# Turning an expert's gathered tokens by transposing DMAs instead of on the matrix engine

## The chip, the core and the metric

The kernel runs on one core of a Trainium2 chip. The core has a matrix engine (PE, with PEld for its weight loads), a vector engine (DVE), a scalar engine (ACT), GpSimd (POOL) and a queue engine (SP), beside 16 DMA engines that they share. PE writes only to PSUM, and other engines copy from there to SBUF. The metric is the device time of one execution in microseconds (us), here the median over several executions.

## The reference

One layer of a diffusion backbone over 2048 tokens of width 1024: a token mixer (convolution heads and HGRN heads), and then a mixture of 16 experts in which each expert picks its 256 best tokens. Only the mixture is touched:

```python
gate, idx = lax.top_k(probs.transpose(0, 2, 1), cap)          # cap = 256, 16 experts
xs = jax.vmap(lambda hb, ib: hb[ib])(h, idx)                  # gathered token rows
hid = (jax.nn.silu(jnp.einsum('becd,edf->becf', xs, p['w_gate']))
       * jnp.einsum('becd,edf->becf', xs, p['w_up']))
out = jnp.einsum('becf,efd->becd', hid, p['w_down']) * gate[..., None].astype(h.dtype)
y = ...zeros((n, d)).at[ib.reshape(-1)].add(ob.reshape(-1, d))
```

## The kernel before

Every float32 product is made of three bf16 products (`triple`, lines 89 to 91): each operand is split in a high half (`hi`, the value rounded to bf16) and a low half (`lo`, what is left over). The token rows lie in HBM as `s_rows`: per token 1024 bf16 high halves, 1024 bf16 low halves and the router's 16 probabilities.

`moe_stage` runs the experts one after another. Each engine has its own program; the first expert and the last are written out (`experts`, `peeled`), and those between are a loop. Engines meet through counters (semaphores) alone. For one expert:

- POOL gathers its 256 rows from `s_rows` into `mrows` (`rows`, two halves `s` of 128 tokens) by two indirect DMAs, about 45 us ahead of their use, and at the end adds the expert's output to `s_y` in HBM by two indirect DMAs (L2294), one for each `s`.
- PE needs the rows with the model width on the partitions. `turn` (L2558) does this for the next expert in two calls: 16 transposes of 128x128 each (L2565) into the PSUM tiles `ptx[0]` (high) and `ptx[1]` (low), after which ACT copies `ptx[0]` into `xhi` (L2325) and DVE copies `ptx[1]` into `xlo` (L2435). `xhi` and `xlo` exist once, so their new contents may be written only after the last gate/up product of the expert that runs (counter `gu_ps`).
- PE runs eight gate/up steps `f` (48 products `pgu` of 256 columns each, L89 to L91) and then four down steps `q` (24 products `pd` of 512 columns each, L2608 to L2610). The first call of `turn` stands after step f = 6, the second after q = 0.
- ACT applies tanh (`thb`, L2345), and ACT and DVE make `fhi` and `flo` of the hidden values. DVE weighs the output (`ysb`, L2467).
- The weights are six blocks `b` of 2 MB in float32 (gate, up, gate, up, down, down), loaded by SP (L2011) into three staging buffers `mwst`. ACT rounds each half block into `mwhi` (L2337), DVE subtracts into `mwlo` (L2440), and after the second half of a block the staging buffer is free and SP may load the block three further on. Blocks 0 to 2 of an expert are loaded and split while the one before it runs. SP therefore issues block 3 of an expert during the down steps of the expert before it, and block 4 a little later.

SP's program is one queue in program order, and each issue waits for its counter:

```python
for b in range(NB):
    wait(sp, w_lo[b % NS], 2 * (e * 2 + b // NS))
    EW.load(sp, e, b)
```

Of the kernel before, what the change touches and what calls it, by code (L numbers as in the profile page):

```python
# [27 lines left out]
P = 128  # L28
# [2144 lines left out]
def moe_stage(nc, K, I, scr, EW, out):  # L2173
# [5 lines left out]
    with nc.cleanup_on_exit(), ExitStack() as ctx:  # L2179
# [30 lines left out]
        oh0_ok, ls_ok = m.sem("oh0_ok"), m.sem("ls_ok")  # L2210
        oh_ok, id_ps, idf_ok, id_ok, idc_ok, gt_ok = (m.sem("oh_ok"), m.sem("id_ps"), m.sem("idf_ok"), m.sem("id_ok"),
                                                      m.sem("idc_ok"), m.sem("gt_ok"))
        got, tx_ps, tx_ok = m.sem("got"), m.sem("tx_ps"), m.sems("tx_ok", 2)
        gu_ps, mth_ok, sg_ok, hid_ok, fhi_ok, flo_ok = (m.sem("gu_ps"), m.sem("mth_ok"), m.sem("msg_ok"), m.sem("hid_ok"),
                                                        m.sem("fhi_ok"), m.sem("flo_ok"))
        d_ps, y_ok, put = m.sem("d_ps"), m.sem("my_ok"), m.sem("put")
# [22 lines left out]
        with nc.Block() as block:  # L2239
            @block.sync  # L2240
            def _(sp):
                def one(e):
                    for b in range(NB):
                        if b < NS and isinstance(e, int) and e == 0:
                            continue
                        if b == NS and isinstance(e, int) and e == 0:
                            wait(sp, got, 32)
                        wait(sp, w_lo[b % NS], 2 * (e * 2 + b // NS))
                        EW.load(sp, e, b)
                peeled(sp, NE, one)  # L2250

                def row_group(g):
                    for t in range(4 * g, 4 * g + 4):
                        sp.dma_start(row_tile(t), scr["y"][t * P:(t + 1) * P, :]).then_inc(yt_in[g], 16)

                sp.dma_start(fg[:], I["final_g"].partition_broadcast(P)).then_inc(fg_in, 16)
                wait(sp, put, LAST * 32)
                for g in range(2):
                    wait(sp, w_lo[g], 2 * (LAST * 2 + 2))
                    row_group(g)  # L2260
                wait(sp, gu_ps, LAST * 8 + 4)
                row_group(3)
                wait(sp, w_lo[2], 2 * (LAST * 2 + 2))
                row_group(2)

            @block.gpsimd
            def _(pool):
                pool.dma_start(g2[:], scr["modrows"][6:8, :].rearrange("a n -> (a n)").partition_broadcast(P))\
                    .then_inc(g2_in, 16)
                nc.gpsimd.memset(pflag[:], 0.0).then_inc(fl_ok, 1)  # L2270

                def carrier():
                    nc.gpsimd.tensor_tensor(pflag[:], pflag[:], pflag[:], ALU.mult).then_inc(fl_ok, 1)  # L2273

                def prep(e, first=False):
                    wait(pool, fl_ok, 1 if first else e * 3 - 1)
                    wait(pool, id_ok, e + 1)
                    wait(pool, tx_ps, e * 4)
                    wait(pool, gt_ok, e)
                    carrier()  # L2280
                    for s in range(2):
                        pool.indirect_dma_start(out=rows32[:, s, :], out_offset=None, in_=scr["rows"],
                                                in_offset=bass.IndirectOffsetOnAxis(ap=idn[:, s:s + 1], axis=0))\
                            .then_inc(got, 16)

                def body(e, nxt):
                    if nxt:
                        prep(e + 1)
                    wait(pool, put, e * 32)
                    for s in range(2):  # L2290
                        wait(pool, y_ok, e * 4 + 2 * s + 2)
                        wait(pool, fl_ok, e * 3 + s + (3 if nxt else 2))
                        carrier()
                        pool.indirect_dma_start(out=scr["y"], out_offset=bass.IndirectOffsetOnAxis(ap=idc[:, s:s + 1], axis=0),  # L2294
                                                in_=ysb[:, s, :], in_offset=None, compute_op=ALU.add).then_inc(put, 16)

                def last(e, nxt):
                    wait(pool, put, e * 32)
                    for s in range(2):
                        pool.indirect_dma_start(out=ygat[:, s, :], out_offset=None, in_=scr["y"],  # L2300
                                                in_offset=bass.IndirectOffsetOnAxis(ap=idn[:, s:s + 1], axis=0))\
                            .then_inc(yg_in, 16)
                    for n, t in enumerate(ORDER):
                        wait(pool, yt_ok, n + 1)
                        pool.dma_start(out[0, t * P:(t + 1) * P, :], row_tile(t)).then_inc(yt_out, 16)
                    wait(pool, yt_out, 16 * NT)
                    for s in range(2):
                        wait(pool, yn_ok, 2 * s + 2)
                        pool.indirect_dma_start(out=out_rows, out_offset=bass.IndirectOffsetOnAxis(ap=idn[:, s:s + 1], axis=0),
                                                in_=ygat[:, s, :], in_offset=None).then_inc(yg_out, 16)  # L2310

                out_rows = out.rearrange("a t d -> (a t) d")
                def prep0(e):
                    prep(0, True)
                    EW.first_low(nc, pool, HEAD_START - 2)

                experts(pool, prep0, body, last)
                wait(pool, yg_out, 32)

            @block.scalar  # L2320
            def _(act):
                def turn(e, j):
                    wait(act, tx_ps, e * 4 + 2 * j + 1)
                    wait(act, gu_ps, e * 8)
                    nc.scalar.activation(xhi[:, 4 * j:4 * j + 4, :], ptx[0][:], ACT.Copy).then_inc(tx_ok[0], 1)  # L2325

                def split(e, r):
# [51 lines left out]
                def body(e, nxt):  # L2379
                    for j in range(8):  # L2380
                        hidden(e, j, nxt)
                        if not nxt and j >= 4:
                            row_squares(2 * j - 8)
                            row_squares(2 * j - 7)
                    for q in range(4):
                        if nxt:
                            if q < 2:
                                turn(e + 1, q)
                            split(e, HEAD_START + 8 + q)
                        else:  # L2390
                            for n in range(8 + 4 * q, min(NT, 12 + 4 * q)):
                                row_squares(n)
                            gathered_squares(q)
                            if q % 2 == 1:
                                gathered_deviation(q // 2)

                def prep0(e):
                    turn(0, 0)
                    turn(0, 1)

                experts(act, prep0, body)

# [1 line left out]
            def _(dve):  # L2404
# [24 lines left out]
                    nc.vector.scalar_tensor_tensor(idn[:], f2[:, :, 1], float(P), f2[:, :, 0], ALU.mult, ALU.add)\  # L2429
                        .then_inc(id_ok, 1)  # L2430

                def turn(e, j):
                    wait(dve, tx_ps, e * 4 + 2 * j + 2)
                    wait(dve, gu_ps, e * 8)
                    nc.vector.tensor_copy(xlo[:, 4 * j:4 * j + 4, :], ptx[1][:]).then_inc(tx_ok[1], 1)  # L2435

                def split(e, r):
# [62 lines left out]
                def body(e, nxt):  # L2500
# [17 lines left out]
                    wait(dve, gt_ok, e + 1)  # L2518
                    for q in range(4):
                        if nxt:  # L2520
                            if q < 2:
                                turn(e + 1, q)
                            split(e, HEAD_START - 1 + 8 + q)
                        else:
                            for n in range(4 + 4 * q, min(NT, 8 + 4 * q)):
                                row_scaled(n)
# [6 lines left out]
                def prep0(e):  # L2533
                    first_list()
                    numbers(0)
                    list_rows(nc, dve, K, 1, NE, ls_ok, 0)
                    turn(0, 0)
                    turn(0, 1)

                experts(dve, prep0, body)  # L2540

# [1 line left out]
            def _(pe):  # L2543
# [11 lines left out]
                        last = nc.tensor.matmul(pid, oneh[:, t, :], Re[:, t, :], start=(t == 0), stop=(t == NT - 1))  # L2555
                    last.then_inc(id_ps, 1)

                def turn(e, j):  # L2558
                    wait(pe, got, e * 32 + 32)
                    for part in range(2):  # L2560
                        wait(pe, tx_ok[part], e * 2 + j)
                        for k in range(4):
                            for s in range(2):
                                c = part * D + (4 * j + k) * P
# [3 lines left out]

                def body(e, nxt):
                    start = isinstance(e, int) and e == 0  # L2570
                    for part in range(2):
                        wait(pe, tx_ok[part], e * 2 + (1 if start else 2))
                    for f in range(8):
                        h, jj = f // 4, f % 4
                        if jj == 0:
# [17 lines left out]
                        last.then_inc(gu_ps, 1)  # L2593
                        if nxt and f == 2:
                            token_list(e + 1)
                        if nxt and f == 6:
                            turn(e + 1, 0)
                    wait(pe, flo_ok, e * 8 + 7)
                    for b in (4, 5):
                        wait(pe, w_lo[b % NS], 2 * (e * 2 + b // NS + 1))  # L2600
                    for q in range(4):
# [8 lines left out]
                            last = nc.tensor.matmul(pd[q % 2][:], fl, whi[:, 4 + c, k, :], start=False,  # L2610
                                                    stop=(k == KD - 1))
                        last.then_inc(d_ps, 1)
                        if nxt and q == 0:
                            turn(e + 1, 1)

                def prep0(e):
                    token_list(0)
                    turn(0, 0)
                    turn(0, 1)

                experts(pe, prep0, body)

# [83 lines left out]
```

## Time and profile before

| | |
|---|---|
| median of 3 runs | 2312.58 us |
| lowest and highest of the runs | 2309.34 and 2317.04 us |
| span of the profiled execution | 2315.0 us, within the runs' range |
| PE busy, DVE busy, ACT busy | 94%, 70%, 45% of the span |
| moved by the DMA engines | 377.14 MB, mean 163 GB/s |
| mean granted clock of PE | 0.971 of full speed |

The span runs from the first to the last instruction of one execution, recorded by the profiler; the record gives no other time for that execution, and the span lies 2.4 us above the median of the runs. Busy time is the union of an engine's instructions; a busy PE isn't PE at its peak, since its products overlap.

### The profile page before, as it was taken

The numbers are of one execution on the slowest core, as the hardware profiler recorded it, in microseconds if no ns is written. First come the engines' busy times: TensorE is split into PE (matmuls) and PEld (weight loads), VectorE is DVE, ScalarE is ACT, GpSimd is POOL, SyncE is SP. The second block draws the span as 40 slices with busy tenths as digits, with TensorE's granted clock in tenths as the row PEclk, the third lists the DMA queues.
The fourth block names the chain that finished last, engine by engine and source line by source line (L and its number), as shares of the span: only waits on it lengthen the run. The fifth ranks groups of instructions, "written<-read, shape, count | busy, mean of one in ns | idle before, by whom it ended". The sixth has DMA issues, their size and how long they took to land. (4 is left out here: it accounts for less than half of the span.)

```text
span 2315.0 us, 38576 instructions
## 1 busy us (share of the span) xinstructions
PE 2187.4 (94%) x14737; PEld 1480.7 (64%) x14885; DVE 1609.4 (70%) x2233; ACT 1041.0 (45%) x1329; POOL 504.9 (22%) x537
## 2 busy tenths in 40 slices
PE   7799999998999999899986999999999999999995
PEld 3444444444878787755534777777777777777773
DVE  2749999785679687865566667666666666666666
ACT  3611011456566666644442444543444444543444
POOL 1710001013657567300012111101111011101111
PEclk9899999999999999899977999999999999999998
DMA  9341002454021111375453776667766766667776
GB/s 345 98 73 37 14 23 87 149 161 124 6 55 50 45 57 24 116 263 165 152 189 137 241 232 230 224 218 227 243 220 211 242 218 240 219 221 233 229 233 266
DMA packets 216931, 377.14 MB, mean 163 GB/s; under 512 B 38147, under 2 KB 79619, under 8 KB 216333
## 3 DMA queue, kind: packets, MB, share of 16 engines
q1 hardware_dynamic: 198702, 317.38, 40.7%
q0 software_dynamic: 16528, 56.47, 9.0%
q10 hardware_dynamic: 1616, 2.16, 0.3%
q8 instruction: 53, 0.87, 0.2%
q14 instruction: 32, 0.26, 0.0%
HBM read 313.44 MB, written 62.54 MB: 162 GB/s over the span
## 5 line engine op out<-in xcount | busy, mean ns | idle before, releaser
L89 PE MATMUL pgu<-xhi,mwhi 128*128 128x256 bf16 x2048 | 558.8, 273 | 0.0
L90 PE MATMUL pgu<-xlo,mwhi 128*128 128x256 bf16 x2048 | 558.7, 273 | 0.0
L91 PE MATMUL pgu<-xhi,mwlo 128*128 128x256 bf16 x2048 | 558.6, 273 | 0.0
L2440 DVE TENSOR_TENSOR mwlo<-mwst,mwhi 128x2048 bf16<-128x2048 f32 x187 | 427.0, 2283 | 0.0
L2337 ACT ACTIVATE mwhi<-mwst 128x2048 bf16<-128x2048 f32 x186 | 350.8, 1902 | 0.1
L2345 ACT ACTIVATE thb<-pgu 128x256 f32<-128x256 f32 x128 | 49.0, 383 | 548.0 <-PE pgu L91 548.0
L676 DVE SCALAR_TENSOR_TENSOR co<-u,taps,co 128x1984 f32<-128x1984 f32 (+22 forms) x120 | 234.1, 1951 | 3.7
L2451 DVE SCALAR_TENSOR_TENSOR thb<-thb,pgu 128x256 f32<-128x256 f32 x128 | 53.8, 421 | 259.0 <-ACT thb L2345 259.0
L2273 POOL TENSOR_TENSOR mpflag<-mpflag 1x1 f32<-1x1 f32 x46 | 37.5, 815 | 846.4 <-DVE ysb L2467 579.4
L89 PEld LDWEIGHTS pgu<-xhi,mwhi 128*128 128x128 bf16 x2048 | 200.5, 98 | 24.6
L90 PEld LDWEIGHTS pgu<-xlo,mwhi 128*128 128x128 bf16 x2048 | 200.6, 98 | 24.5
L91 PEld LDWEIGHTS pgu<-xhi,mwlo 128*128 128x128 bf16 x2048 | 200.5, 98 | 23.5
L2610 PE MATMUL pd<-mwhi,flo 128*128 128x512 bf16 x511 | 193.9, 379 | 0.8
L2609 PE MATMUL pd<-mwlo,fhi 128*128 128x512 bf16 x497 | 188.9, 380 | 2.9 <-DVE flo L2459 1.4
L2608 PE MATMUL pd<-mwhi,fhi 128*128 128x512 bf16 x481 | 182.9, 380 | 3.3 <-DVE ysb L2467 3.1
L1521 PEld LDWEIGHTS pout<-E,KX 128*128 128x128 f32 (+2 forms) x1024 | 151.3, 181 | 32.6 <-POOL KX L1100 8.4
L1521 PE MATMUL pout<-E,KX 128*128 128x32 f32 (+2 forms) x1024 | 145.1, 234 | 13.0 <-POOL KX L1100 8.0
L2467 DVE SCALAR_TENSOR_TENSOR ysb<-pd,gate,g 128x512 f32<-128x512 f32 x64 | 47.9, 749 | 84.5 <-PE pd L2610 84.5
L1498 PE MATMUL pj<-hhi,wst 128*128 128x512 bf16 (+1 forms) x300 | 104.0, 372 | 1.6 <-PEq L422 1.6
L1498 PE MATMUL pout<-hhi,wst 128*128 128x512 bf16 (+1 forms) x284 | 95.8, 364 | 0.2
L557 ACT ACTIVATE jb<-pout 128x512 f32<-128x512 f32 (+1 forms) x54 | 31.4, 591 | 136.9 <-PE pout L91 119.6
L1308 DVE TENSOR_TENSOR_SCAN B<-segm,E 128x512 f32<-128x512 f32 (+1 forms) x40 | 52.1, 1303 | 58.6 <-ACT E L1156 58.6
(397 smaller groups left out, 4399.2 us busy)
## 6 DMA issues: line engine op xcount, KB each, us to landing
mwst<-in_w_gate SPq DMA_DIRECT2D x32, 2048.0 KB, 9.1
mwst<-in_w_up SPq DMA_DIRECT2D x32, 2048.0 KB, 7.9
mwst<-in_w_down SPq DMA_DIRECT2D x32, 2048.0 KB, 7.9
wst<-in_w_in SPq DMA_DIRECT2D x28, 512.0 KB, 6.1
big<-in_ada_w SPq DMA_DIRECT2D x5, 2048.0 KB, 14.6
s_rows<-row SPq DMA_DIRECT2D x16, 520.0 KB, 5.8
u<-in_ada_w SPq DMA_DIRECT2D x8, 1024.0 KB, 6.1
xt<-in_x SPq DMA_DIRECT2D x16, 512.0 KB, 4.4
```

The lines of the kernel that those rows point to most:

```text
L89: nc.tensor.matmul(out, lh, rh, start=(first and k == 0), stop=False)
L90: nc.tensor.matmul(out, lh, rl, start=False, stop=False)
L91: ins = nc.tensor.matmul(out, ll, rh, start=False, stop=(last and k == n - 1))
L676: nc.vector.scalar_tensor_tensor(o, i, taps[:, c, k:k + 1], o, ALU.mult, ALU.add).then_inc(tap_ok, 1)
L1498: ins = nc.tensor.matmul(pj[i % 2][:, 0:n], w, x, start=(mm == 0), stop=(mm == 3 * KD - 1))
L1521: ins = nc.tensor.matmul(pat[0:keys, n * CH:(n + 1) * CH], KX[:, p, n * P:n * P + keys], E[:, p, n * CH:(n + 1) * CH], start=True, stop=True)
L2337: nc.scalar.activation(whi[:, b, ks], wst[:, b % NS, ks], ACT.Copy).then_inc(w_hi, 1)
L2440: nc.vector.tensor_tensor(wlo[:, b, ks], wst[:, b % NS, ks], whi[:, b, ks], ALU.subtract)\
L2451: nc.vector.scalar_tensor_tensor(thb[:, p], thb[:, p], 1.0, pgu[p][:, 0, :], ALU.add, ALU.mult)\
L2608: nc.tensor.matmul(pd[q % 2][:], fh, whi[:, 4 + c, k, :], start=(k == 0), stop=False)
L2609: nc.tensor.matmul(pd[q % 2][:], fh, wlo[:, 4 + c, k, :], start=False, stop=False)
L2610: last = nc.tensor.matmul(pd[q % 2][:], fl, whi[:, 4 + c, k, :], start=False, stop=(k == KD - 1))
```

## The change

For the first expert nothing changes. For experts 1 to 15, PE's two calls of `turn`, ACT's two copies into `xhi` and DVE's two copies into `xlo` are taken out. In their place SP issues four transposing DMAs (`turned`): each reads 128 tokens by 1024 bf16 values (256 KB) of `mrows` and writes them turned into `xhi` or `xlo`, SBUF to SBUF. They stand in SP's queue right behind the load of block 3 of that expert and ahead of the loads of blocks 4 and 5. They wait for the gather of the expert (`got`) and for the last gate/up product of the expert before it (`gu_ps`). PE starts the gate/up steps when all four have landed (`xt_in`, 64 counts for an expert), and POOL overwrites `mrows` only after that.

```diff
             @block.sync
             def _(sp):
+                def turned(e):
+                    wait(sp, gu_ps, e * 8)
+                    sp.sem_inc(x_free, 1)
+                    sp.wait_ge(x_free, 1)
+                    for part, x in enumerate((xhi, xlo)):
+                        for s in range(2):
+                            sp.dma_start_transpose(x[:, :, s * P:(s + 1) * P], rows[:, s, part * D:(part + 1) * D])\
+                                .then_inc(xt_in, 16)
+
                 def one(e):
                     for b in range(NB):
                         if b < NS and isinstance(e, int) and e == 0:
                             continue
-                        if b == NS and isinstance(e, int) and e == 0:
-                            wait(sp, got, 32)
+                        if b == NS:
+                            wait(sp, got, e * 32 + 32)
                         wait(sp, w_lo[b % NS], 2 * (e * 2 + b // NS))
                         EW.load(sp, e, b)
+                        if b == NS and not (isinstance(e, int) and e == 0):
+                            turned(e)
                 peeled(sp, NE, one)
...
                 def prep(e, first=False):
-                    wait(pool, tx_ps, e * 4)
+                    if not first:
+                        wait(pool, tx_ps, 4)
+                        wait(pool, xt_in, e * 64 - 64)
...
                     for q in range(4):
                         if nxt:
-                            if q < 2:
-                                turn(e + 1, q)
                             split(e, HEAD_START + 8 + q)
...
                 def body(e, nxt):
                     start = isinstance(e, int) and e == 0
-                    for part in range(2):
-                        wait(pe, tx_ok[part], e * 2 + (1 if start else 2))
+                    if start:
+                        for part in range(2):
+                            wait(pe, tx_ok[part], 1)
+                    else:
+                        wait(pe, xt_in, e * 64)
...
                         if nxt and f == 2:
                             token_list(e + 1)
-                        if nxt and f == 6:
-                            turn(e + 1, 0)
...
                         last.then_inc(d_ps, 1)
-                        if nxt and q == 0:
-                            turn(e + 1, 1)
```

(The `turn` calls are taken out of ACT's and of DVE's loop over `q` in the same way.)

SP's queue in the experts' loop, from the load of block 3 (`in_w_up`) to the end of the loop. Before:

```order
L2011 DMA mwst<-in_w_gate 128x8x512
L75 ISA
L2011 DMA mwst<-in_w_up 128x8x512
L2011 DMA mwst<-in_w_down 128x8x512 x2
L81 REGISTER_ALU
L81 COMPARE_AND_BRANCH
```

And now:

```order
L2011 DMA mwst<-in_w_up 128x8x512
L75 REGISTER_ALU
L2249 DMA_TRANSPOSE xhi<-mrows 128x8x128 x2
L2249 DMA_TRANSPOSE xlo<-mrows 128x8x128 x2
L2011 DMA mwst<-in_w_down 128x8x512 x2
L81 REGISTER_ALU
L81 COMPARE_AND_BRANCH
```

The four transposing DMAs lie between the loads of block 3 and block 4.

DVE's program in the same loop, from the last `flo` of an expert to the weighing of the second down step. Before:

```order
L2459 TENSOR_TENSOR flo<-hb,fhi 128x256
L75 ISA
L75 REGISTER_ALU
L2435 COPY xlo<-ptx 128x1024
L75 REGISTER_ALU
L2440 TENSOR_TENSOR mwlo<-mwst,mwhi 128x2048
L75 REGISTER_ALU
L2467 SCALAR_TENSOR_TENSOR ysb<-pd,gate,g 128x512
L75 REGISTER_ALU
L2435 COPY xlo<-ptx 128x1024
L75 REGISTER_ALU
L2440 TENSOR_TENSOR mwlo<-mwst,mwhi 128x2048
```

And now:

```order
L2469 TENSOR_TENSOR flo<-hb,fhi 128x256
L75 REGISTER_ALU
L2450 TENSOR_TENSOR mwlo<-mwst,mwhi 128x2048
L75 REGISTER_ALU
L2477 SCALAR_TENSOR_TENSOR ysb<-pd,gate,g 128x512
L75 REGISTER_ALU
L2450 TENSOR_TENSOR mwlo<-mwst,mwhi 128x2048
```

Both copies of `xlo` are gone, and the subtraction that frees the staging buffer for block 3 (the first `mwlo` here) follows `flo` at once.

## Rows read from the trace of the kernel before

**Rows 1.** The page: PE's busy tenths and granted clock, 40 slices.
```profile
PE   7799999998999999899986999999999999999995
PEclk9899999999999999899977999999999999999998
```

**Rows 2.** Busy time of each engine in one expert's period (stretches).
```profile
core 0: us, PE busy (x) PEld busy (x) DVE busy (x) ACT busy (x) POOL busy (x), PEclk, DMA share, GB/s
1376.10:1441.00 64.90, 64.74 (x528) 49.15 (x529) 42.62 (x48) 29.03 (x30) 7.70 (x8) 1.00 0.69 226
```

**Rows 3.** Chain that ended last, in order of time: start, us, what.
```profile
1289.58 0.89 PE ptx L2565 x16
1300.89 0.89 PE ptx L2565 x16
...
2197.20 0.89 PE ptx L2565 x16
2208.51 0.89 PE ptx L2565 x16
```

**Rows 4.** Timeline of ACT around one expert's end: start, us, instruction, idle before.
```profile
1414.04 0.38 ACT L2345 ACTIVATE thb<-pgu 128x256 f32<-128x256 f32 x1 [2.75 <-PE pgu L91]
...
1419.28 0.38 ACT L2345 ACTIVATE thb<-pgu 128x256 f32<-128x256 f32 x1 [2.75 <-PE pgu L91]
...
1425.41 0.38 ACT L2345 ACTIVATE thb<-pgu 128x256 f32<-128x256 f32 x1 [3.65 <-PE pgu L91]
...
1452.55 1.90 ACT L2337 ACTIVATE mwhi<-mwst 128x2048 bf16<-128x2048 f32 x1
...
1463.03 1.90 ACT L2337 ACTIVATE mwhi<-mwst 128x2048 bf16<-128x2048 f32 x1
```

**Rows 5.** Timeline of DVE at the same expert's end.
```profile
1428.83 0.42 DVE L2459 TENSOR_TENSOR flo<-hb,fhi 128x256 bf16<-128x256 f32 x1
1429.16 0.68 DVE L2435 COPY xlo<-ptx 128x1024 bf16<-128x1024 bf16 x1
1429.76 2.28 DVE L2440 TENSOR_TENSOR mwlo<-mwst,mwhi 128x2048 bf16<-128x2048 f32 x1
...
1437.34 2.28 DVE L2440 TENSOR_TENSOR mwlo<-mwst,mwhi 128x2048 bf16<-128x2048 f32 x1
```

**Rows 6.** Timeline of SP: issues of block 3 (up) and block 4 (down).
```profile
1432.07 0.37 SPq L2011 DMA_DIRECT2D mwst<-in_w_up  x1
1439.64 16.52 SPq L2011 DMA_DIRECT2D mwst<-in_w_down  x2
```

**Rows 7.** Stretches, columns as in rows 2, while block 3 loads.
```profile
1436.00:1438.00 2.00, 2.00 (x11) 0.91 (x10) 1.33 (x2) 1.46 (x1) 0.41 (x1) 1.00 1.05 406
1438.00:1440.00 2.00, 2.00 (x11) 0.94 (x10) 1.61 (x1) 0.00 (x0) 1.84 (x2) 1.00 0.60 223
```

**Rows 8.** DMA issues from 1432 to 1433 us: size, us to landing.
```profile
mwst<-in_w_up SPq DMA_DIRECT2D x1, 2048.0 KB, 7.9
```

**Rows 9.** Timeline of PE: a late product of q = 0, the first of the next expert.
```profile
1429.74 0.38 PE L2608 MATMUL pd<-mwhi,fhi 128*128 128x512 bf16 x1
...
1446.83 0.27 PE L89 MATMUL pgu<-xhi,mwhi 128*128 128x256 bf16 x1
```

**Rows 10.** DMA queues from 685 to 692 us: packets, MB, share of 16 engines.
```profile
DMA packets 1056, 0.26 MB, mean 37 GB/s; under 512 B 1056, under 2 KB 1056, under 8 KB 1056
q1 hardware_dynamic: 1056, 0.26, 17.6%
```

**Rows 11.** POOL's first scatter; its queue's first packets, 1444.5 to 1445.5 us.
```profile
1439.82 1.62 POOL L2294 DMA_INDIRECT s_y<-ysb,idc  x1 [0.16 <-issue]
...
q0 software_dynamic: 14, 0.06, 32.1%
```

**Rows 12.** DMA issues of the whole span: size, median us to landing.
```profile
s_v<-jb POOLq DMA_DIRECT2D x18, 256.0 KB, 2.7
...
cc<-in_c SPq DMA_DIRECT2D x1, 4.0 KB, 1.7
```

More of the change, by code:

```diff
@@ L2212, in moe_stage @@
                                                       m.sem("idc_ok"), m.sem("gt_ok"))
-        got, tx_ps, tx_ok = m.sem("got"), m.sem("tx_ps"), m.sems("tx_ok", 2)
+        got, tx_ps, tx_ok, xt_in = m.sem("got"), m.sem("tx_ps"), m.sems("tx_ok", 2), m.sem("xt_in")
+        x_free = m.sem("x_free")
         gu_ps, mth_ok, sg_ok, hid_ok, fhi_ok, flo_ok = (m.sem("gu_ps"), m.sem("mth_ok"), m.sem("msg_ok"), m.sem("hid_ok"),
@@ L2321, in _, with turn @@
             def _(act):
-                def turn(e, j):
-                    wait(act, tx_ps, e * 4 + 2 * j + 1)
-                    wait(act, gu_ps, e * 8)
+                def turn(j):
+                    wait(act, tx_ps, 2 * j + 1)
                     nc.scalar.activation(xhi[:, 4 * j:4 * j + 4, :], ptx[0][:], ACT.Copy).then_inc(tx_ok[0], 1)
@@ L2397, in prep0 @@
                 def prep0(e):
-                    turn(0, 0)
-                    turn(0, 1)
+                    turn(0)
+                    turn(1)
                 experts(act, prep0, body)
@@ L2430, in numbers, with turn @@
                         .then_inc(id_ok, 1)
-                def turn(e, j):
-                    wait(dve, tx_ps, e * 4 + 2 * j + 2)
-                    wait(dve, gu_ps, e * 8)
+                def turn(j):
+                    wait(dve, tx_ps, 2 * j + 2)
                     nc.vector.tensor_copy(xlo[:, 4 * j:4 * j + 4, :], ptx[1][:]).then_inc(tx_ok[1], 1)
@@ L2520, in body @@
                         if nxt:
-                            if q < 2:
-                                turn(e + 1, q)
                             split(e, HEAD_START - 1 + 8 + q)
@@ L2536, in prep0 @@
                     list_rows(nc, dve, K, 1, NE, ls_ok, 0)
-                    turn(0, 0)
-                    turn(0, 1)
+                    turn(0)
+                    turn(1)
                 experts(dve, prep0, body)
@@ L2556, in token_list, with turn @@
                     last.then_inc(id_ps, 1)
-                def turn(e, j):
-                    wait(pe, got, e * 32 + 32)
+                def turn(j):
+                    wait(pe, got, 32)
                     for part in range(2):
-                        wait(pe, tx_ok[part], e * 2 + j)
+                        wait(pe, tx_ok[part], j)
                         for k in range(4):
@@ L2612, in body @@
                         last.then_inc(d_ps, 1)
-                        if nxt and q == 0:
-                            turn(e + 1, 1)
                 def prep0(e):
                     token_list(0)
-                    turn(0, 0)
-                    turn(0, 1)
+                    turn(0)
+                    turn(1)
                 experts(pe, prep0, body)
```

## The prediction

> **What bounds the kernel now.** The page comes first: from the 23rd slice on, the experts, PE is busy in nine tenths and more of every slice at nine tenths and more of the full clock [rows 1]. The stretch of one expert's period says the same closer: PE is busy 64.74 of 64.90 us, DVE 42.62, ACT 29.03, and the DMA engines have a share of 0.69 [rows 2]. So whatever is taken off PE there is gained, as long as nothing new makes PE wait. The chain of work in order of time then shows the pieces that the change removes on that very path: 16 transposes at a time, 0.89 us, the first at 1289.58 and the last at 2208.51 us, two for each of experts 1 to 15, 30 pieces in all [rows 3].
>
> **What is removed.** ACT's tanh follows each gate/up step, so its starts are PE's step: 5.24 us from 1414.04 to 1419.28 and 6.13 us over the step with a turn in it, 0.89 more [rows 4]. This agrees with the chain, so I take 30 x 0.89 = 26.7 us, 1.78 us for each expert. ACT's two copies and DVE's two aren't on the path. They are worth nothing by themselves, but one of them stands ahead of the subtraction that frees the staging buffer, which matters below: from 1429.16 to 1429.76, 0.60 us [rows 5].
>
> **What is added, and when it can start.** I put the new DMAs on the time axis of the expert shown. SP issues block 3 at 1432.07 [rows 6], when DVE has ended the subtraction of 1429.76 [rows 5]. After the change the first turn (0.89) lies no longer ahead of it, nor does DVE's copy (0.60): block 3 is issued at 1430.6. The last gate/up product, for which `turned` also waits, is over by then (tanh of the last step starts at 1425.41 [rows 4]), and so is the gather. SP goes on to the four transposing DMAs at about 1431. Their packets stand behind those of block 3 in SP's queue. That load saturates the DMA engines (share 1.05, 406 GB/s), and its packets end at about 1439.2 (0.60 of the stretch from 1438 on) [rows 7]; it lands 7.9 us after its issue, at 1440.0 [rows 8], 0.8 after its last packet. Moved by 1.49 us, its packets end at 1437.7, and the turning begins there.
>
> **When it is needed.** The next expert's first product starts at 1446.83 [rows 9], and after the change 1.78 earlier, at 1445.05. With 0.8 us for landing, the turning of 1 MB (4 x 256 KB) may last T = 1445.05 - 0.8 - 1437.7 = 6.5 us before PE waits. Each us beyond costs 15 us in all, and at T = 8.3 the whole gain is used up.
>
> **How long the turning takes.** The trace has no transposing DMA, so T is bounded. From below: at the rate of the weight loads, 406 GB/s [rows 7], 1.05 MB take 2.6 us. From above: if every DMA were paid alone, with nothing overlapped, 4 x 2.7 us as the 256 KB DMAs land [rows 12], 10.8 us. If it were paid in its 32 blocks of 128x128, each as the smallest DMA in the trace, 1.7 us [rows 12], 54 us. Between them stand the smallest packets that SP's queue moves: 1056 packets of about 256 bytes take 17.6% of 16 engines for 7 us, 18.7 ns each [rows 10]. A row of a 128x128 block of bf16 is just such a piece, 256 bytes, and 1 MB is 4096 of them, 256 on each engine: 4.8 us. I take T = 4.8 us, by that nearest row. The turning then ends at 1442.5 and lands at 1443.3, 1.7 us before PE needs it. Against the load of block 3 itself nothing is lost, as it stands in front.
>
> The rows give a moved MB between 2.6 and 4.8 us, by the size of its packets. The Trainium skill (Advanced Engine Details and Errata, X-Bar Transpose (TRN2)) says that transposing DMAs are as fast as regular ones and expects 350 to 400 GB/s; by that T would be an estimated 2.6 to 3.0 us, and the sum would be the same, with more to spare. No transposing DMA in this trace can show whether it holds.
>
> **What lies beside it.** The other work of the DMA engines is POOL's first scatter: it is issued at 1439.82, but its packets show only from 1444.5 on [rows 11], 1442.7 after the change. So a turning of 4.8 us is just over when they come; a longer one has to share. Behind the turning in SP's queue waits block 4, issued at 1439.64 when the subtraction of 1437.34 is over [rows 5, 6], now due at 1437.9. Even if SP is held until 1443.3, block 4 lands some 8 us later at 1451.3, and ACT first reads it at 1463.03 - 1.78 = 1461.3 [rows 4]: 10 us to spare. Block 3 is read from 1452.55 on [rows 4] and lands at 1438.5. The engines' DMA share rises from 0.69 [rows 2] by 4.8 of 63 us, to about 0.8 of the shorter period. On PE the next cover is thin but unmoved: the last `flo` ends at 1429.25 [rows 5], and the product group that needs it starts at 1429.74 [rows 9]; the turn that goes stands ahead of both, and the copies that go stand behind. All this costs nothing.
>
> **The sum.** 2315.0 - 26.7 = 2288.3 us for the profiled execution. Its span lies 2.4 us above the median of the runs, so for the median 2312.6 - 26.7 = 2285.9 us, 1.2% faster.
>
> **The rivals.**
> - A short stall, chance 0.16: T lies between 6.5 and 8.3 us or a little above, because the turning's packets are dearer than plain ones or because its end meets the scatter. For it speaks how near all the times lie to each other (1.7 us); against it that the scatter comes late. At T = 7.4 PE waits 0.9 us for each expert: 2285.9 + 15 x 0.9 = 2299 us.
> - The four DMAs don't overlap, chance 0.20, and this is the one that ends on the other side. Each 256 KB transfer is paid with its landing, 2.7 us [rows 12], and the first can only start when block 3 has landed at 1438.5: 1438.5 + 10.8 = 1449.3, a wait of 4.3 us at the first product. 2285.9 + 15 x 4.3 = 2350 us. It decides from a wait of 1.78 us on, so from 2.1 us for each of the four. For it speaks that a turned block can't be written before its rows are all read; against it that plain DMAs of one queue follow each other with no gap: the engines are at 1.05 share in the middle of a load [rows 7].
> - Turning block by block, chance 0.10. 32 blocks of 128x128, each at 1.7 us [rows 12], end at 1437.7 + 54 = 1491.7, a wait of 47 us for each expert and 2990 us in all; SP is held too, and blocks 4 and 5 come late inside the same wait. Against it speaks that each instruction carries 128x1024 values and so should be spread over the engines as any other. The Trainium skill (VectorE: DVE Perf Modes, The three transpose paths) gives 1309 ns for a 128x128 block by DMA against 390 ns on TensorE, and its Rules for kernel authors prefer TensorE where PSUM will do; if that price were paid 32 times, it would be an estimated 42 us for an expert and some 2810 us in all. That TensorE's own price in this stream is far lower is what the trace shows: 0.89 us for 16 of them, 56 ns each [rows 3].
> - No gain at all, chance 0.02: the time taken off PE comes back as another wait. PE has no other wait in the period that could grow (0.16 us idle of 64.90 [rows 2]), so this needs a cover that I have missed.
>
> **How the numbers follow.** The likeliest case, hidden turning, has 0.52; its own range is the runs' spread about 2286, 2281 to 2292 us. The whole range takes in the short stall and most of the four DMAs one by one (2350 at the full 2.7 us, less if they overlap in part): 2280 to 2348 us, with the lower parts of the second rival some 0.82. What is left out is the rest of it and the block-by-block case. Within 0.3% of before (2306 to 2320, about what a measurement can tell from no change) means a wait of 1.3 to 2.2 us: 0.05 of the short stall and the 0.02 of no gain, 0.07. Faster: 0.52 + 0.09 of the short stall = 0.61. Slower: 0.02 of it, 0.20 and 0.10, 0.32.
>
> **What would show it.** Right: no `ptx` in the experts' loop, a period of 63.0 us instead of 64.8, the four transposing DMAs issued at once behind block 3 and landing within 13 us of their issue, and no idle time ahead of an expert's first `pgu` product. A wait of PE there, put down to SP's DMAs, would show the rivals, and its length says which: under 2 us, about 4, or tens. The step that I trust least is T. If PE's clock falls after such waits, they cost more than their length: it shows 0.7 in the two slices ahead of the experts, where PE isn't full either [rows 1].

## The result, and the profile after

| | before | changed |
|---|---|---|
| median of 20 runs | 2313.35 us | 2322.3 us |
| lowest and highest | 2308.88, 2319.23 | 2312.59, 2330.18 |
| span of the profiled execution | 2315.0 us | 2313.3 us |

The ratio of the changed kernel to the one before is 1.0037, with a 95% interval from 1.0028 to 1.0046: slower by 0.4%, where 1.2% faster was forecast. The profiled execution of the changed kernel is one of its quickest (2315.06 us, when the median is 2322.3), so the profile shows the mechanism and not quite the median's amount of it.

The page of the changed kernel answers to [rows 1]: its PE line and its granted clock, unchanged to the eye in the experts' slices.

```profile
PE 2162.5 (93%) x14405; PEld 1446.0 (63%) x14405; DVE 1595.7 (69%) x2203; ACT 1013.5 (44%) x1299; POOL 505.6 (22%) x537
...
PE   7799999998999999899976999999999999999995
...
PEclk9899999999999999899987999999999999999998
```

PE has lost 24.9 us of busy time (2187.4 before), about what was taken away. The waits of PE, longest first in total, show where it went (waiting instruction, releaser, us in total, times, longest):

```profile
PE pgu L89 <- DMA xlo<-mrows: 27.7, 15, 2.7
```

Before there was no such line. Every one of the 15 experts now starts with a wait for the last turning DMA. One of them on PE's timeline (idle time and its releaser at the end of the row), which answers to [rows 9]:

```profile
1437.66 0.38 PE L2619 MATMUL pd<-mwhi,flo 128*128 128x512 bf16 x1
1439.62 0.28 PE L89 MATMUL pgu<-xhi,mwhi 128*128 128x256 bf16 x1 [1.59 <-DMA xlo<-mrows]
```

SP's and POOL's timelines at the same expert answer to [rows 6] and to the POOL row of [rows 11]:

```profile
1423.41 0.37 SPq L2011 DMA_DIRECT2D mwst<-in_w_up  x1
1423.99 7.69 SPq L2249 DMA_TRANSPOSE xhi<-mrows  x2
1431.72 4.43 SPq L2249 DMA_TRANSPOSE xlo<-mrows  x2
1436.26 12.71 SPq L2011 DMA_DIRECT2D mwst<-in_w_down  x2
```

```profile
1430.87 1.62 POOL L2308 DMA_INDIRECT s_y<-ysb,idc  x1 [0.16 <-issue]
```

The last product of the down steps starts at 1437.66, and in their pace (0.22 us from start to start) the next expert's first would have followed at 1437.9, 14.5 us after block 3's issue (1423.41), as the prediction's axis had it (1430.6 to 1445.05). The DMA queues in single microseconds (packets, MB, share of 16 engines; q1 is SP's queue, q0 POOL's), from 1432, 1434, 1435 and 1438 us on:

```profile
q1 hardware_dynamic: 1055, 0.26, 129.3%
...
q0 software_dynamic: 31, 0.13, 86.3%
q1 hardware_dynamic: 41, 0.01, 8.9%
...
q0 software_dynamic: 44, 0.18, 90.8%
q1 hardware_dynamic: 46, 0.01, 9.2%
...
q1 hardware_dynamic: 735, 0.25, 139.7%
```

At 1432 the turning moves 1055 packets of 256 bytes in a microsecond. Then the scatter's 4 KB packets come (from 1433.3 on), and the turning falls to 41 and 46 a microsecond, here about one for each packet of the scatter; at other experts of this trace it is fewer (from 1630.57 to 1631.57 it is 10 beside 49). At 1438 it is quick again. In all its packets last from 1430.6 to 1438.8, 8.2 us, of which some 3 are spent at this crawl.

### The profile page after: what moved, and what is told of

It is laid out like the page before. It is cut to its first block and busy times, and to the rows that moved or that the text cites. A ratio compares the mean times of both kernels' runs of the same rounds, so it can differ in the third digit from the quotient of the medians.

```text
span 2313.3 us, 37650 instructions
## 1 busy us (share of the span) xinstructions
PE 2162.5 (93%) x14405; PEld 1446.0 (63%) x14405; DVE 1595.7 (69%) x2203; ACT 1013.5 (44%) x1299; POOL 505.6 (22%) x537
## 5 line engine op out<-in xcount | busy, mean ns | idle before, releaser
L89 PE MATMUL pgu<-xhi,mwhi 128*128 128x256 bf16 x2048 | 559.1, 273 | 27.7 <-DMA xlo<-mrows 27.7
L2617 PE MATMUL pd<-mwhi,fhi 128*128 128x512 bf16 x512 | 194.6, 380 | 4.5 <-DVE ysb L2477 3.3
L2618 PE MATMUL pd<-mwlo,fhi 128*128 128x512 bf16 x512 | 194.6, 380 | 0.0
L1521 PEld LDWEIGHTS pout<-E,KX 128*128 128x128 f32 (+2 forms) x1024 | 146.4, 177 | 31.5 <-POOL KX L1100 7.7
L1498 PE MATMUL pout<-hhi,wst 128*128 128x512 bf16 (+1 forms) x304 | 101.4, 363 | 0.0
## 6 DMA issues: line engine op xcount, KB each, us to landing
mwst<-in_w_down SPq DMA_DIRECT2D x32, 2048.0 KB, 10.2
```

The source lines that it names most:

```text
L89: nc.tensor.matmul(out, lh, rh, start=(first and k == 0), stop=False)
L1498: ins = nc.tensor.matmul(pj[i % 2][:, 0:n], w, x, start=(mm == 0), stop=(mm == 3 * KD - 1))
L1521: ins = nc.tensor.matmul(pat[0:keys, n * CH:(n + 1) * CH], KX[:, p, n * P:n * P + keys], E[:, p, n * CH:(n + 1) * CH], start=True, stop=True)
L2617: nc.tensor.matmul(pd[q % 2][:], fh, whi[:, 4 + c, k, :], start=(k == 0), stop=False)
L2618: nc.tensor.matmul(pd[q % 2][:], fh, wlo[:, 4 + c, k, :], start=False, stop=False)
```

## The experiments

Each run gives the median, and the ratio to the kernel before with its 95% interval, from runs of both on the same chip, 4 to 10 executions of each run's kernel. Two theories for the wait were tested first: that the turning is hindered by the scatter, and that it is slow by itself.

**Without turning.** `turned` isn't issued, and the waits for it are gone.

```diff
-                        if b == NS and not (isinstance(e, int) and e == 0):
-                            turned(e)
...
-                    else:
-                        wait(pe, xt_in, e * 64)
```

> Leaves out the turning for experts 1 to 15: neither PE's transposes nor the DMAs, so experts 1 to 15 use the first expert's tokens. It prices what the change removes. Every theory expects the 30 x 0.89 us read from the chain: 2313 - 27 = 2286 us, a ratio to before of 0.988, and no wait of PE ahead of an expert's first product.

2285.65 us, ratio 0.9881 (0.9866 to 0.9897). The 26.7 us that the removed transposes were priced at are right to within the runs' spread.

**Scatter after the turning.** One wait is added on POOL, and nothing else is changed.

```diff
                     wait(pool, put, e * 32)
+                    wait(pool, xt_in, e * 64 + 64)
                     for s in range(2):
                         wait(pool, y_ok, e * 4 + 2 * s + 2)
```

> The change as it is, but POOL issues an expert's first scatter only after the next expert's turning has landed. Nothing else moves. Theory A (scatter against turning): the turning lands 4.8 + 0.8 us after block 3's last packets, about 1435.5, ahead of PE at 1438: PE's wait is gone, 2286 us, ratio to before 0.988. Theory B (the turning is slow by itself): nothing changes, PE waits about 1.8 to 2.5 us for each expert, 2315 to 2325 us.

2286.98 us, ratio 0.9887 (0.987 to 0.9904): the whole gain is there. Two stretches of its trace, columns as in [rows 2], from 1376 and from 1431 us on:

```profile
1376.00:1441.00 65.00, 65.00 (x516) 49.13 (x515) 42.14 (x48) 27.22 (x28) 7.00 (x10) 1.00 0.81 255
...
1431.00:1436.50 5.50, 5.50 (x28) 2.47 (x26) 3.27 (x3) 0.00 (x0) 0.00 (x0) 1.00 1.13 234
```

PE is never idle. The scatter is issued at 1437.82, and one microsecond of the turning, from 1433 on, shows the queue q1 alone:

```profile
1437.82 1.62 POOL L2309 DMA_INDIRECT s_y<-ysb,idc  x1 [0.52 <-issue]
```

```profile
q1 hardware_dynamic: 912, 0.23, 112.9%
```

Followed microsecond by microsecond, the 256-byte packets run from 7.3 to 12.2 us after block 3's issue (1424.18), with no scatter beside them: 4.9 us for 1 MB (4096 packets, so 836 in a microsecond in the mean), where 4.8 was forecast. The theory that the turning is slow by itself is gone.

**Everything twice.** As the last, with four more turning DMAs into a buffer that isn't read (`ygat`, idle until the end).

```diff
-                    for part, x in enumerate((xhi, xlo)):
+                    for part, x in ((0, xdup), (1, xdup2), (0, xhi), (1, xlo)):
```

> As the run with the later scatter, and each turning is done twice: four more transposing DMAs into a buffer that nobody reads, ahead of the four that count. It gives the price of 1 MB turned with no scatter beside it. Theory A (4.8 us for 1 MB): 9.6 us after block 3's packets, landing about 1440.2, a wait of 2.3 us for each expert, about 2320 us. Theory B (9 us for 1 MB): landing near 1449, a wait of 11 us for each expert, about 2450 us.

2378.53 us, ratio 1.0275 (1.0255 to 1.0295), 58 us more than the first theory's number and 72 less than the second's. The packets last 10.8 us for 2 MB, so 5.4 for 1 MB: near the first theory. PE's waits:

```profile
PE pgu L89 <- DMA xlo<-mrows: 60.0, 15, 4.8
```

They are 4.0 us for each expert, where the first theory said 2.3: that is 25 us of the 58. What it had left out beside that is PE's clock. Stretches behind one wait of 4.2 us, columns as in [rows 2] (the clock is the third number from the end):

```profile
1450.00:1454.00 4.00, 4.00 (x21) 1.77 (x19) 2.40 (x2) 0.00 (x0) 0.00 (x0) 1.00 1.02 194
1454.00:1458.50 4.50, 0.59 (x3) 0.09 (x1) 0.92 (x2) 0.00 (x0) 0.00 (x0) 0.94 1.03 173
1458.80:1462.80 4.00, 3.96 (x19) 2.87 (x20) 0.00 (x0) 0.00 (x0) 3.23 (x4) 0.50 1.05 376
1462.80:1466.80 4.00, 4.00 (x30) 3.20 (x29) 0.00 (x0) 0.00 (x0) 0.15 (x1) 0.76 1.04 252
1466.80:1470.80 4.00, 4.00 (x39) 3.59 (x38) 3.20 (x4) 2.49 (x3) 0.00 (x0) 1.00 0.69 136
```

After the idle stretch the clock is at half its level (1.2 instead of 2.4 GHz) for about 6 us, and PE starts 19 products where 39 fit. Before this, PE had worked at the full clock without a gap. From the first product behind this wait to the next expert's (1458.84 to 1528.88) there are 70.0 us, 7.0 more than the 63.05 without turning (64.83 - 1.78): the next wait is 4.0 of them, and the lower clock the other 3.0.

**Turning ahead of block 3.** The wait for the gather moves up to block 2's load, and `turned` ahead of block 3's.

```diff
-                        if b == NS:
+                        start = isinstance(e, int) and e == 0
+                        if b == (NS if start else NS - 1):
                             wait(sp, got, e * 32 + 32)
+                        if b == NS and not start:
+                            turned(e)
                         wait(sp, w_lo[b % NS], 2 * (e * 2 + b // NS))
                         EW.load(sp, e, b)
-                        if b == NS and not (isinstance(e, int) and e == 0):
-                            turned(e)
```

> The turning stands ahead of block 3's load in SP's queue (the wait for the gather stands a little earlier, ahead of block 2's load). Theory A (scatter against turning, 5 us for 1 MB by itself): SP issues the four DMAs as the last gate/up product ends, near 1417 on the axis of the changed kernel's expert, their packets follow block 2's at 1423 and end near 1428, before the scatter comes at 1433; no wait of PE, about 2286 us, ratio to before 0.988. Theory B (the four DMAs pay about 2.7 us each): packets end near 1434, also hidden, and 2286 us. Theory C (block 3 then lands too late for ACT, which reads it near 1445 on that axis): block 3's packets come 5 us later, end near 1436 and share with the scatter; 9 us to spare, so no cost expected; if it were late, ACT would wait for w_up.

2288.61 us, ratio 0.9876 (0.9856 to 0.9897). It beats both kernels and can't be told from the one with the later scatter. SP's timeline:

```profile
1417.89 0.37 SPq L2011 DMA_DIRECT2D mwst<-in_w_gate  x1
1419.49 6.55 SPq L2249 DMA_TRANSPOSE xhi<-mrows  x2
1426.09 2.69 SPq L2249 DMA_TRANSPOSE xlo<-mrows  x2
1428.96 0.44 SPq L2011 DMA_DIRECT2D mwst<-in_w_up  x1
```

SP is held for 9.3 us, and block 3 is issued at 1428.96. Its packets end near 1436.3, it lands 8.4 us after its issue, at 1437.4, and ACT first reads it at 1445.67, so the later load costs nothing, as expected.

**Turning behind block 4.** The condition `b == NS` at the call of `turned` becomes `b == NS + 1`.

> The turning stands behind block 4's load instead of block 3's: block 4 is issued near 1430.7 on the changed kernel's axis, its 2 MB (5.3 us alone) meet the scatter, and end near 1440; the turning's packets follow. Theory A: they end near 1445 and meet the second scatter (issued as the fourth down step is weighed, packets from about 1443 on), so they land between 1446 and 1450: a wait of 8 to 12 us for each expert against the need at 1438, plus the lower clock after such a wait (some 3 us as in the doubled run): 2286 + 15 x 13 = about 2480 us. A theory in which the place in the queue doesn't matter, because the chip moves the transposing DMAs' packets beside the loads', expects 2322 us as in the change.

2479.07 us, ratio 1.0712 (1.0687 to 1.0736); about 2480 was expected. The waits of PE:

```profile
PE pgu L89 <- DMA xlo<-mrows: 161.1, 15, 11.2
```

10.7 us for each expert, and the period is 12.9 us longer than without turning ((2479.07 - 2285.65) / 15); of the rest, 2.2 us, the clock is a part: it is granted at 0.61 in the 4 us behind the wait that ends at 1477.2, and at 1.00 from 1481.2 on. A place in the queue later by one 2 MB load is worth 10 us here against the changed kernel. One load alone is some 5 us; but block 4's load meets the first scatter, and the turning behind it the second, as was expected. In the microseconds from 1472 and 1473 on the turning is between its first packets (1469) and its last (1476):

```profile
q0 software_dynamic: 47, 0.19, 96.3%
...
q0 software_dynamic: 52, 0.20, 102.1%
q1 hardware_dynamic: 5, 0.00, 0.8%
```

In the first of them it moves no packet at all, so one for each of the scatter's is at most what it gets.

**ACT issues.** The four DMAs are issued by ACT behind its last `fhi`, in a queue of their own.

```diff
+                            if q == 0:
+                                turned(e + 1)
                             split(e, HEAD_START + 8 + q)
```

> ACT issues the four transposing DMAs, behind its last fhi of an expert, instead of SP; they then have a queue of their own and don't stand behind block 3. Theory A (a short packet has to wait for one long packet of the other queue): beside block 2's and block 3's 2 KB packets the turning goes at about a fifth of its rate, alone at its own 19 ns a packet; packets end near 1432, in time for PE. What it may cost is ACT itself: if the issuing engine is held while the DMAs queue, as SP is for 11 us in the change, ACT's splits of the next blocks come up to 11 us late, DVE's weighing stands behind them, and PE's down steps wait for it: 2290 to 2400 us, with ACT's DMA_TRANSPOSE rows long. If an engine is only held 1.3 us for each where nothing stands ahead in its queue, ACT loses 5.3 us, which its idle time before the next tanh covers: about 2286 us.

2334.19 us, ratio 1.0091 (1.0072 to 1.0111). PE's longest waits are now others:

```profile
PE pd L2617 <- DVE ysb L2477: 38.2, 17, 3.0
```

ACT's timeline, and DVE's and PE's first instruction that waited:

```profile
1425.11 3.54 ACTq L2331 DMA_TRANSPOSE xhi<-mrows  x1
1428.68 6.68 ACTq L2331 DMA_TRANSPOSE xlo<-mrows  x2
```

```profile
1437.41 2.29 DVE L2450 TENSOR_TENSOR mwlo<-mwst,mwhi 128x2048 bf16<-128x2048 f32 x1 [8.46 <-ACT mwhi L2348]
```

```profile
1440.42 0.39 PE L2617 MATMUL pd<-mwhi,fhi 128*128 128x512 bf16 x1 [2.66 <-DVE ysb L2477]
```

ACT is held from 1423.7 to 1435.4, its splits stand behind that, DVE's weighing behind them, and PE waits for the weighing: the first of the two outcomes that were foreseen for ACT. The queues beside each other (q1 is SP's, q10 now ACT's), in the microseconds from 1429, 1431, 1433 and 1435 on:

```profile
q10 hardware_dynamic: 1119, 0.28, 127.9%
...
q1 hardware_dynamic: 179, 0.37, 103.6%
...
q1 hardware_dynamic: 179, 0.37, 120.2%
q10 hardware_dynamic: 73, 0.02, 8.2%
...
q1 hardware_dynamic: 176, 0.36, 92.4%
q10 hardware_dynamic: 170, 0.04, 19.2%
```

Alone the turning moves 1119 packets in a microsecond. Beside the 2 KB packets of a weight load it passes about one for each of the load's from 1433.5 to 1436.5 (402 beside 429). But from 1430.25 to 1433.25 it moves none at all beside 457 of the load's, and none from 1424 to 1427, though its first DMA was issued at 1423.74 and its third at 1428.68. No run shows why. Theory A had expected a fifth of its rate all through and its last packet near 1432; it comes at 1438.6.

**Half rows.** Each scatter becomes two of 2 KB rows.

```diff
-                        pool.indirect_dma_start(... in_=ysb[:, s, :], in_offset=None, compute_op=ALU.add).then_inc(put, 16)
+                        for c in range(2):
+                            pool.indirect_dma_start(..., element_offset=c * SEG,
+                                                    in_=ysb[:, s, c * SEG:(c + 1) * SEG], ...).then_inc(put, 16)
```

> The change as it is, but each scatter is issued as two DMAs of half rows (2 KB instead of 4 KB for each token), so that the scatter's packets are half as long. Theory A (the two queues alternate packet by packet, so a short packet waits for one long one): while both are there, the turning passes one packet for each of the scatter's as before, but twice as many in a us, about 80 instead of 40 to 47; over the scatter's 4 us that wins some 0.4 us for each expert, and the time comes out between 2310 and 2322 us, unless POOL's two further issues (1.6 us each) put the scatter's first packets elsewhere. If POOL joins two half rows in one packet, nothing changes. A theory in which the scatter stops the turning altogether for its own length, whatever its packets, expects 40 to 47 packets a us and 2322 us.

2322.7 us, ratio 1.0047 (1.0026 to 1.0067), no change in time. The scatter's packets are now 2 KB (91 packets and 0.18 MB in one microsecond), but it comes in two parts, the second while the turning still runs or just after, and 54 packets of the turning beside those 91 are no clean sign of 80. Shorter stretches of the same trace show both: from 1571.28 to 1571.78 the turning passes 49 beside 45 (98 a microsecond, over twice the 41 to 46 beside 4 KB packets), from 1444.00 to 1444.75 only 23 beside 67 (31 a microsecond). The run doesn't settle whether the packets' length sets the pace, nor whether the two queues alternate at all.

**The changed kernel again**, for a second profile.

> The changed kernel again, for a second profile. Theory A: PE waits 1.5 to 3 us ahead of each expert, the turning's packets nearly stop for as long as the scatter's are there. Where the execution takes longer than the 2313.3 us span profiled first, the granted clock falls to half for some us after some of the waits, as it does behind each 4 us wait of the doubled run; if instead all the waits were just longer at a full clock, the clock is not part of it.

2323.8 us, ratio 1.0036 (1.0017 to 1.0055); the profiled span is 2325.0 us. PE's waits are nearly the same, but of the 15 stretches of 6 us behind each expert's first product two are at a lower clock, and in the first profile one (the stretches shown start 0.5 us behind that product):

```profile
PE pgu L89 <- DMA xlo<-mrows: 29.3, 15, 3.3
```

```profile
1382.95:1388.95 6.00, 6.00 (x58) 5.37 (x56) 0.57 (x2) 1.02 (x2) 0.87 (x1) 1.00 1.05 321
1449.46:1455.46 6.00, 6.00 (x33) 4.38 (x32) 0.00 (x0) 0.00 (x0) 0.00 (x0) 0.56 1.05 312
...
2102.94:2108.94 6.00, 6.00 (x42) 4.76 (x40) 0.00 (x0) 0.00 (x0) 0.79 (x1) 0.72 1.04 317
```

The clock fell after the longest wait of each profile, 2.7 us in the first (the first product at 2220.97) and 3.3 us in the second (1448.99), and after one of 2.0 us (2102.47). After the 27 other waits, of 1.3 to 2.2 us, it stayed at the full clock.

## Why the prediction was wrong

**What bounds the kernel, and what is removed: right.** 30 x 0.89 = 26.7 us came out as 27.5 in the run without turning (2313.17 - 2285.65).

**When it can start and when it is needed: right.** The turning's packets start 7.2 us after block 3's issue (7.1 forecast), and the next expert's first product would have started 14.5 us after it (14.45 forecast).

**How long the turning takes by itself: right.** 4.9 us with the scatter out of the way, 5.4 in the doubled run, against 4.8 from the 256-byte packets of [rows 10].

**What lies beside it: this step failed**, as it was put: "a turning of 4.8 us is just over when they come; a longer one has to share". Two things in it were wrong. The scatter's first packets came 2.2 to 3.7 us after its issue (the first scatters in the two profiles of the changed kernel; 2.4 at the one shown), not 4.7, so 0.9 to 2.4 us before a turning of 4.9 us was over. And sharing wasn't priced: I took it as slower by some share, when it stops the short packets almost wholly. The turning gets at most about one packet for each of the scatter's, and a packet of 256 bytes against one of 4 KB leaves it a twentieth of its pace for as long as the scatter lasts (41 to 46 against 836 in a microsecond): 8.2 us instead of 4.9. That is the "short stall" rival's mechanism with a larger size (its T of 7.4, and the 8.3 at which it put the break-even). It was given 0.16; that its end would meet the scatter was named there, but its price wasn't worked out, though the rows had it: q0's 14 packets in a third of 16 engines' microsecond [rows 11] are 0.37 us each, 20 times the 18.7 ns of a short one [rows 10]. A scatter's 128 rows of 4 KB are then 128 x 0.37 / 16 = 3.0 us of the engines' time by estimate, and the turning was stretched by 3.3: about the whole scatter. The run with the later scatter shows that the scatter is the whole cause of the wait. That the two queues alternate packet by packet isn't shown: beside the scatter and beside a load there were also whole microseconds with no packet of the turning.

**The sum.** From the chain, an expert's period before is 64.83 us ((2208.51 - 1300.89) / 14 [rows 3]) and 1.78 less without turning. In the two profiles of the changed kernel the first products of experts 1 and 15 lie 911.4 and 916.9 us apart, 65.1 and 65.5 us for each period, so the wait costs 2.1 and 2.5 us, more than the 1.78 gained. 15 x 0.3 = 5 us and 15 x 0.7 = 10 us frame the measured 9. By the prediction's own rule a turning of 8.2 us makes PE wait 8.2 - 6.5 = 1.7 us, 2311 us in all; so the mis-sized T brings the time back to that of before, and the last 11 us come on top. The bare waits (27.7 and 29.3 us in the rows) are a little longer than 15 x 1.7. In the first profile they are the whole difference from the run without turning (spans of 2313.3 and 2285.1 us). In the second a part is the clock: the two periods that begin with a lower clock are 67.5 and 66.8 us, 2.4 and 1.7 us above the usual 65.1. The last remark of the prediction, that the clock might fall after a wait, was right. What the rest of the median's 2322.3 us is made of isn't shown.

**The rivals.** Four DMAs one by one (2350 us) and block by block (2990 us) are refuted: 1 MB needs 4.9 us, not 10.8 or 54. SP being held was seen rightly as harmless (block 4 has 10 us to spare), and it is: with the later scatter SP is held for 10.2 us (12.2 in the changed kernel) and nothing is lost. On the rule of the Trainium skill (Advanced Engine Details and Errata, X-Bar Transpose (TRN2)), that transposing DMAs are as fast as regular ones, this case disagrees in the rate: 1 MB in 4.9 us is 214 GB/s, against 400 for the weight loads here and the 350 to 400 that the Trainium skill expects; it agrees with plain packets of the same 256 bytes. The other figure of the Trainium skill (VectorE: DVE Perf Modes, The three transpose paths), 1309 ns for a 128x128 block, isn't what a block costs in a row of them: 4.9 us for 32 are 153 ns each.

**What stays open.** Why the first scatter's packets come 2.2 to 3.7 us after its issue in the changed kernel and about 5 us after it before the change. Where a weight load ran at that time (before, without turning, turning ahead) it was 4.6 to 5.5 us; where short packets ran, less. In the changed kernel itself the second scatter of an expert, issued while block 4 loads, takes 4.2 to 5.5 us. No run varies this alone. Nor is it shown why the turning sometimes moves no packet beside another queue, and what decides whether the clock falls after a wait of 2 us.

## What to carry to other kernels

Before a transfer is called hidden, list what else is in the DMA engines in its window and how much of their time that work takes: a stream of 256-byte packets got at most about one for each packet of the other queue, so beside 4 KB packets it nearly stopped (41 to 46 in a microsecond, 1055 alone), and it ended 3.3 us late, by about the 3.0 us of the other transfer. The remedy was order and not speed: the same four DMAs one place earlier in the queue turned 0.4% slower into 1.2% faster. And keep such DMAs on an engine that can be held, since their issue blocks it until they are nearly through: with the later scatter SP came free at 1434.9 and the last packets at 1436.4, and ACT in its place cost 47 us.

## What was unexpected of the hardware

- A stream of short packets got at most about one for each packet of another queue, and at times none: 41 to 46 in a microsecond beside 31 to 44 of 4 KB, 0 beside 47 when the turning stood behind block 4, 1055 alone.
- A transposing DMA holds the engine that issues it: 1.3 us for 256 KB when the queue is empty, 3.7 us in the mean of the first two behind a 2 MB load, 11.6 us for all four on ACT.
- An idle stretch of 4 us on PE was followed by about 6 us at 1.2 GHz, one of 2.7 and one of 3.3 us by 4 to 6 us at it, and of 28 waits between 1.3 and 2.2 us only one, of 2.0.
